# Retention stage of a hybrid layer rebuilt: one lag table, GLU tiles between the heads, column sums, and an out projection begun with the state-space half

## The reference

```python
def ab_mixer(...):        # layer 0
    ql, kl, vl, gl, ul = jnp.split(h_lat @ w_in, cuts, axis=-1)
    r = retention_mixer(...)      # 4 heads of 128; decay exp(log_gamma * |i-j|), both directions, latents start
                                  # from the context's state; rms over the head; times silu(g)
    s = s5_mixer(...)             # 32 groups of a diagonal state space, then gelu, then GLU:
                                  #   y * sigmoid(y @ glu_w + glu_b)
    return jnp.concatenate([r, s], axis=-1) @ w_out
```

## Time and profile before

| | us |
|---|---|
| median of 3 runs (1980.96 to 1985.2) | 1985.0 |
| the profiled execution's own time | 1991.38 |
| its span, first to last instruction | 1989.6 |
| TensorE busy in it | 1875.2 (94%) |
| VectorE busy | 1226.2 (62%) |
| ScalarE busy | 733.2 (37%) |
| last `ab_out` matmul ends, from the start of the span | 761.5 |

### The profile page before, as it was taken

The page is one execution under the profiler, slowest core; times in us unless marked ns, Lnnn a source line. Parts: engine busy times, 40 slices in busy tenths (PEclk is TensorE's granted clock), DMA queues, the critical chain, the costliest instruction groups (busy, mean ns, idle before and its releaser), DMA issues.

```text
span 1989.6 us, 25349 instructions
## 1 busy us (share of the span) xinstructions
PE 1875.2 (94%) x9624; PEld 1557.9 (78%) x9624; DVE 1226.2 (62%) x2021; ACT 733.2 (37%) x1006; POOL 62.6 (3%) x39
## 2 busy tenths in 40 slices
PE   6999999999886689999999999999999999989998
PEld 2788888877786367888888778888887996689998
DVE  4777567779998454776676377764334334545554
ACT  2432122247666434322132342212224323444443
POOL 0000000110000010000000200000010000010001
PEclk8999999989998798999999999999998998989999
DMA  7454454321100122543553344443222520024543
GB/s 288 164 196 152 181 200 179 113 86 64 43 33 33 53 89 81 211 179 142 199 196 120 113 162 178 167 169 127 87 82 85 207 90 1 1 106 148 185 175 126
DMA packets 39859, 259.10 MB, mean 130 GB/s; under 512 B 4688, under 2 KB 5840, under 8 KB 14704
## 3 DMA queue, kind: packets, MB, share of 16 engines
q1 hardware_dynamic: 39792, 258.23, 35.5%
HBM read 257.17 MB, written 1.05 MB: 130 GB/s over the span
## 4 chain that ended last, share of the span: by engine, by line
PE 84%; DVE 10%; ACT 3%; issue 2%; DMA 1%; SPq 0%; DVEq 0%; ACTq 0%
PE ps_all L1528 25%; PE ps_all L1532 25%; PE ps_all L1529 25%; PE ps_all L1840 2%; PE bank L1851 2%; DVE w_lo L914 2%; PE bank L1576 1%; DMA start_scale<-in_w_scale 1%; PE ps_all L1830 1%; PE bank L1830 1%; ACT w_hi L551 1%; PE bank L1879 1%; DVE cp L444 1%; PE bank L1770 1%; DVE stat L1289 1%
## 5 line engine op out<-in xcount | busy, mean ns | idle before, releaser
L1528 PE MATMUL ps_all<-a_hi,w_lo 128*128 128x512 f32 (+1 forms) x1808 | 666.3, 369 | 29.0 <-ACT a_hi L659 14.0
L1532 PE MATMUL ps_all<-a_lo,w_hi 128*128 128x512 f32 (+1 forms) x1808 | 661.1, 366 | 0.2 <-DVE a_lo L1053 0.2
L1529 PE MATMUL ps_all<-a_hi,w_hi 128*128 128x512 f32 (+1 forms) x1808 | 660.7, 365 | 0.0
L914 DVE TENSOR_TENSOR w_lo<-w_raw,w_hi 128x2048 fp32r<-128x2048 f32 (+3 forms) x184 | 376.3, 2045 | 169.5 <-ACT w_hi L551 168.3
L551 ACT ACTIVATE w_hi<-w_raw 128x2048 fp32r<-128x2048 f32 (+3 forms) x183 | 313.5, 1713 | 350.0 <-PE ps_all L1532 347.0
L1528 PEld LDWEIGHTS ps_all<-a_hi,w_lo 128*128 128x128 f32 x1808 | 347.3, 192 | 88.8 <-issue 16.1
L1532 PEld LDWEIGHTS ps_all<-a_lo,w_hi 128*128 128x128 f32 x1808 | 347.0, 192 | 57.1 <-DVE a_lo L1053 4.1
L1529 PEld LDWEIGHTS ps_all<-a_hi,w_hi 128*128 128x128 f32 x1808 | 347.7, 192 | 52.2
L926 DVE SCALAR_TENSOR_TENSOR mod_junk<-mod_raw,cond 128x1024 bf16<-128x1024 f32 x256 | 302.5, 1218 | 4.7 <-ACT cond L579 2.7
L1528 PE MATMUL ps_all<-g_hi,w_lo 128*128 128x512 f32 (+1 forms) x704 | 258.3, 367 | 0.8 <-DVE w_lo L914 0.8
L1532 PE MATMUL ps_all<-g_lo,w_hi 128*128 128x512 f32 (+1 forms) x704 | 258.1, 367 | 0.0
(11 more groups left out here) (209 smaller groups left out, 1564.7 us busy)
## 6 DMA issues: line engine op xcount, KB each, us to landing
w_raw<-in_tiles SPq DMA_DIRECT2D x118, 1024.0 KB, 4.8
mod_raw<-in_w_mod SPq DMA_DIRECT2D x64, 1024.0 KB, 4.8
w_raw<-in_tiles SPq DMA_DIRECT2D x32, 768.0 KB, 4.0
w_raw<-in_tiles SPq DMA_DIRECT2D x32, 640.0 KB, 3.7
start_raw<-in_w_mod SPq DMA_DIRECT2D x4, 1024.0 KB, 16.0
start_scale<-in_w_scale SPq DMA_DIRECT2D x4, 1024.0 KB, 20.1
bias<-in_na_bias SPq DMA_DIRECT2D x2, 1536.0 KB, 8.3
cond<-in_cond SPq DMA_DIRECT2D x2, 1024.0 KB, 6.0
```

The costliest lines, as they stand in the source:

```text
L914: nc.vector.tensor_tensor(w_lo[:, slot, 0:size], w_raw[:, slot, 0:size], w_hi[:, slot, 0:size].bitcast(F32), ALU.subtract).then_inc(lo_rea ...
L1528: pe.matmul(dst, w[1], x[0], start=start, stop=False)
L1529: pe.matmul(dst, w[0], x[0], start=False, stop=False)
L1532: return pe.matmul(dst, w[0], x[1], start=False, stop=stop_)
```

## The change

- One plane of lags i-j (512 wide, `lag`) replaces the six. It is loaded before the loop, the logits earlier still, and log_gamma is worked out beside ffn0.down1. For each head: decay[:,0] = exp(min(lf*d, -lb*d)) plus the identity on the diagonal blocks, and the cross term exp(lf*d + 256 lf) + exp(-lb*d + 256 lb), so three exponentials and one scaled copy on ScalarE, and one min, one add and two 128-wide adds on VectorE. Each head has buffers of its own, so that ScalarE no longer waits for VectorE's masks.
- In the loop ScalarE does gelu(2b-1) ahead of the kernel rows; the last gate tile is evacuated one turn earlier; in turn 7 VectorE's split of the second `glu` weights moves from ahead of rotate(15) to behind the split of y, and the scores of head 0 go between the last two outputs.
- The `glu` tiles run between the heads, tile 1 into bank[2] and bank[0]; the scores go to ps[1] and bank[1].
- The sum of squares is a column sum (16 matmuls with one column for each of the four heads' 4 blocks), one Sqrt over 16 columns, one reciprocal, and a spread by four 128-wide matmuls a head.
- `ab_out` tiles 0 and 1 begin with the state-space half of k; heads lie in a_hi blocks 4 to 7, y in 0 to 3. Both first weights are split ahead of the tail's end.

```diff
@@ SyncE
             if segment == "ffn0.down0":
+                sp.dma_start(lgam, i["decay"]).then_inc(ret_sem["gam_in"], 16)
             if segment == "ret_in":
+                sp.wait_ge(pe_done, BASE["s5_in"])
+                sp.dma_start(lag[:], i["lags"]).then_inc(ret_sem["loads"], 16)
...
-                if segment == "glu":
-                    sp.wait_ge(s5_sem["y"], 16)
-                    sp.dma_start(lags[:].rearrange("p a b -> p (a b)"), i["lags"]).then_inc(ret_sem["loads"], 16)
-                    sp.dma_start(lgam[:], i["decay"]).then_inc(ret_sem["loads"], 16)
@@ ScalarE
+                def exponentials(hd):
+                    nc.scalar.activation(decay_of[hd][:, 1, :], lag[:], ACT.Exp, bias=lg[5][:, hd:hd + 1], scale=lg[3][:, hd:hd + 1])
+                    nc.scalar.activation(cross_of[hd], lag[:], ACT.Exp, bias=lg[5][:, 4 + hd:5 + hd],
+                                         scale=lg[4][:, 4 + hd:5 + hd]).then_inc(R["cross"], 1)
+                    act.wait_ge(R["least"], hd + 1)
+                    nc.scalar.activation(decay_of[hd][:, 0, :], decay_of[hd][:, 0, :], ACT.Exp).then_inc(R["exp2"], 1)
...
                 for b in range(8):
+                    if b:
+                        gelu(2 * b - 1)
                     kernel_rows(2 * b)
                     kernel_rows(2 * b + 1)
-                    if b:
-                        gelu(2 * b - 1)
...
+                    if b == 7:
+                        act.wait_ge(S["c"], 8)
+                        slopes(0)
                     gelu(2 * b)
...
                         evacuate(6)
+                        evacuate(7)
+                exponentials(0)
                 gelu(15)
-                evacuate(7)
...
+                for hd in range(1, 4):
+                    slopes(hd)
+                    exponentials(hd)
+                keep(0)
+                split_hi(BASE["ab_out"], 2048, 0)
+                sigmoids(0)
+                keep(1)
+                keep(2)
+                sigmoids(1)
+                split_hi(BASE["ab_out"] + 1, 2048, 1)
+                nc.scalar.activation(warm[:], eps[:], ACT.Sqrt)
+                keep(3)
+                act.wait_ge(R["sum"], 4)
+                nc.scalar.activation(hstd[:], bank[1][:, 0:16], ACT.Sqrt, bias=eps[:, 0:1], scale=D / P).then_inc(R["std"], 1)
                 for hd in range(4):
+                    act.wait_ge(R["mixed"], hd + 1)
+                    nc.scalar.activation(a_hi[:, 4 + hd, :], heads[:, hd, :], ACT.Copy).then_inc(R["cast"], 1)
@@ VectorE
+                mask(0)
+                weigh(0)
                 dve.wait_ge(S["gelu"], 16)
...
+                split_lo(BASE["glu"] + 1, width("glu"), 1)
+                mask(1)
+                weigh(1)
+                mask(2)
+                mask(3)
+                weigh(2)
+                split_lo(BASE["ab_out"], 2048, 0)
+                gated_head(0)
+                weigh(3)
+                y_mix(0)
+                gated_head(1)
+                gated_head(2)
+                y_mix(1)
+                split_lo(BASE["ab_out"] + 1, 2048, 1)
+                gated_head(3)
+                dve.wait_ge(R["std"], 1)
+                nc.vector.reciprocal(hrstd[:], hstd[:]).then_inc(R["rstd"], 1)
@@ TensorE
+                    else:                              # b == 7, after outputs(14)
...
+                        head_scores(0)
                     outputs(2 * b + 1)
...
+                head_scores(1)
+                head_out(0)
+                pe.wait_ge(R["y_split"], 1)
+                glu_tile(0)
+                head_scores(2)
+                head_out(1)
+                head_scores(3)
+                head_out(2)
+                pe.wait_ge(S["rot"], 16)
                 pe.wait_ge(S["gelu"], 16)
...
+                glu_tile(1)
+                head_out(3)
+                pe.wait_ge(R["p"], 4)
                 for hd in range(4):
...
+                    head_sum(hd)
+                out_tile(0, (4, 5))
+                pe.wait_ge(ps_free[1], (BASE["glu"] + 1) // 2 + 1)
+                head_spread(0)
+                head_spread(1)
+                out_tile(0, (6, 7))
+                head_spread(2)
+                pe.wait_ge(R["std"], 1)
+                head_spread(3)
+                out_tile(1, (4, 5, 6, 7))
+                out_tile(0, (0, 1, 2, 3))
+                out_tile(1, (0, 1, 2, 3))
+                for j in range(2, 4):
+                    pair_tile_from("ab_out", j)
```

More of the change, by code:

```diff
@@ L330, in program @@
         ret_sem = {n: sem("ret_" + n) for n in (
-            "loads", "qk", "swapped", "rope", "exp1", "exp2", "gam", "mask", "s", "p", "o", "osq", "kept", "sum", "ln", "std",
-            "y_split", "mix")}
+            "loads", "gam_in", "qk", "swapped", "rope", "gam", "exp1", "slope", "least", "cross", "exp2", "mask", "s", "p", "o",
+            "osq", "kept", "gated", "sum", "std", "rstd", "spread", "mixed", "cast", "mix", "y_split", "ymix")}
         na_sem = {n: sem("na_" + n) for n in (
@@ L606, in step @@
                 def step(t, slot, first=False):
-                    if not (isinstance(t, int) and t == tiles - 1):
+                    if segment == "ab_out" and t == 0:
+                        pass
+                    elif not (isinstance(t, int) and t == tiles - 1):
                         split_hi(BASE[segment] + t + 1, width(segment), 1 - slot)
@@ new lines, in head_out, with head_sum @@
+                def head_out(hd):
+                    pe.wait_ge(R["p"], hd + 1)
+                    if hd:
+                        pe.wait_ge(R["kept"], hd)
+                    for t in (0, 2, 3, 1):
+                        b = 0 if t < 2 else 256
+                        mm = pe.matmul(ps_sum[:, b:512], vtok[:, t, hd * P:(hd + 1) * P], scores[:, t, b:512],
+                                       start=(t == 0), stop=(t == 1))
+                    mm.then_inc(R["o"], 1)
+                def head_sum(hd):
+                    pe.wait_ge(R["osq"], hd + 1)
+                    for t in range(4):
+                        mm = pe.matmul(bank[1][:, 4 * hd + t:4 * hd + t + 1], hsq[hd][:, t * P:(t + 1) * P], mean_c[:],
+                                       start=True, stop=True)
+                    mm.then_inc(R["sum"], 1)
@@ new lines, in head_spread @@
+                def head_spread(hd):
+                    pe.wait_ge(R["rstd"], 1)
+                    if hd == 2:
+                        pe.wait_ge(R["kept"], 4)
+                    for t in range(4):
+                        mm = pe.matmul(spread_to[hd][:, t * P:(t + 1) * P],
+                                       hrstd[:, 4 * hd + t:4 * hd + t + 1].broadcast_to([P, P]),
+                                       const[:, C_IDENT:C_IDENT + P], start=True, stop=True)
+                    mm.then_inc(R["spread"], 1)
@@ new lines, in out_tile @@
+                def out_tile(j, ks):
+                    n = BASE["ab_out"] + j
+                    pe.wait_ge(lo_ready, n + 1)
+                    pe.wait_ge(ps_free[j], n // 2)
+                    w = [x[:, j].rearrange("p (k m f) -> p k m f", k=KT, m=2) for x in (w_hi, w_lo)]
+                    for k in ks:
+                        if k < 4:
+                            pe.wait_ge(R["mix"], k + 1)
+                        else:
+                            pe.wait_ge(R["ymix"], k - 3)
+                        for m in range(2):
+                            mm = three(ps[j][:, m, :], [x[:, k, m] for x in w], (a_hi[:, (k + 4) % 8, :], a_lo[:, (k + 4) % 8, :]),
+                                       k == 4, k == 3)
+                    if k == 3:
+                        mm.then_inc(pe_done, 1)
@@ L1775, in mixer0 @@
-                head_sum(3)
-                pe.wait_ge(R["ln"], 4)
-                pe.wait_ge(R["y_split"], 1)
-                for j in range(2):
-                    pair_tile("glu", j, 4, 4)
-                for j in range(4):
-                    pair_tile("ab_out", j, 8, 0, lambda k: pe.wait_ge(R["mix"], k + 1) if j == 0 else None)
+                head_scores(1)
[3 more added lines that the diff above has]
+                head_scores(2)
```

247 lines of the change are left out of this document (127 added, 120 removed).

## The result

The changed kernel takes 1958.4 us (median of 4 runs, 1958.26 to 1960.32); the kernel before, run on the same chip beside it, took 1985.1 (4 runs, 1980.96 to 1989.07). The ratio is 0.9858, with a 95% interval of 0.9839 to 0.9877, so 1.4% faster. The prediction was 1956.0, with a range from 1947 to 1970.

What follows compares the result with a forecast made beforehand. TensorE, 94% busy, bounds the kernel; only 78 of the mixer tail's 115 us are work. Tail 29.2 plus loop 1.5 is 30.7, minus 1.7 for handoffs gives 29: 1985 - 29 = 1956, range 1947 to 1970.

Steps and rivals of the forecast that it cites:

- The loop: Loop turn 5: VectorE's split no longer waits 1.46 us for ScalarE's w_hi, as gelu moves into idle time; -1.5.
- Moved preparation: Small operations and loads moved to ffn0.down1 fit beside busy TensorE; cost 0, or 2 us without that cover.
- Steps 1 to 3: Tail's start: turn_back(15) done at 640.5 instead of 644.4, outputs(15) ends at 643.0, p1 at 645.8, before 664.2.
- Steps 4 to 6: Tail's heads: scores 1 take 4.2 after 2.8 idle, `glu` tile 0 without a wait, one 2.1 us gap left.
- Step 7: Tail from 666.1: scores 3 through `ab_out` without a break, 66.2 us, ending at 732.3.
- the 1.7 us taken off for handoffs: Taken off the summed 30.7 us gain for some twenty handoffs of nearly 0.1 each left out; leaves 29.
- five signs of the text: New trace: p1 near 644, last `ab_out` matmul near 731, one 2 us idle, no w_hi wait, half clock until about 650.
- A: Tail: short gaps keep TensorE's clock down from scores 1 to value product 2, 21 us more, 1977; chance 0.12.
- B: Tail's heads: product, keep and weigh stay serial, nothing of `glu` hidden; +6.4, 1962; chance 0.13.
- C: Tail: VectorE and ScalarE are always early, the full bound, 1947 to 1950; chance 0.07.
- D: Tail: waits for p2, kept and p3 bring the clock down, `ab_out` stays cold; 53 more, 2038; chance 0.02.
- E: Tail's start: some new wait holds it, only hidden `glu` tiles and first split gained; 1970; chance 0.06.

Runs made afterwards that it cites:

- two edits: Changed kernel plus a second buffer for weighed scores (two heads in flight) and column sums laid between first `ab_out` blocks: 1952.3 us, ratio 0.9813.

## Why the prediction was right

Predicted for the difference was 29.0 us, measured 27.85 in the stage and 26.7 in the medians. By its steps, in positions 0.7 us later than it gave them (turn 0 is 2.2 later, turn 5 took off 1.5):

- **The loop, -1.5.** -1.43 from the split of turn 4 to that of turn 5, and the wait came back when the order was undone.
- **Moved preparation, 0.** Held: turn 0 starts at 468.10 in one execution of the changed kernel, and TensorE was busy throughout where the preparation lies.
- **Steps 1 to 3.** turn_back(15) 641.3 (predicted 641.2), outputs(15) 643.1 (643.7), p1 646.63 (646.5). The whole ordering of ScalarE and VectorE in turn 7 held, down to the table switches: gelu(14) ended at 640.75, and the load behind it took 1.28 with the next operation 1.30 after its start. The drain that the Trainium skill adds ("ScalarE: Activation LUTs", What ACT_TABLE_LOAD costs) isn't there, and the 3 us later end that it gave did not come.
- **Steps 4 to 6.** Scores 1 took 4.37 (4.2) after 3.61 us idle (2.8), scores 2 waited for nothing, kept head 0 was ready at 660.9, 0.8 before TensorE asked, and the one gap was 2.08 (2.1).
- **Step 7, mis-sized.** Predicted were 66.2 us from scores 3 to the end, measured 69.3 (666.53 to 735.83). Scores 3 cost 4.37, not 3.6 (in the kernel before, such a set took 4.00, from 673.88 to 677.88, after 2.17 us idle, as the row below shows in part: I had priced only its first four matmuls from there); the column sums 4.47, not 3.6; `ab_out` 46.2, not 43.6, for half clock at its start; the spreads 3.6, not 4.4. The step says "from 666.1 TensorE has work without a break", which was so, and took from it that the clock stays up, which was not so. That the forecast came this close is in part luck: the 1.7 us taken off for handoffs covered for more than half of this error, and no such handoffs show in step 7, where TensorE is busy for 5.00 of every 5 us from 676 to 691.

```profile
676.18 1.91 PE L1753 MATMUL bank<-qk 128*128 128x256 f32 x4
```

- **No wait for ymix, mix or kept.** None came. Of the five signs of the text, three held: p1 (644.4 in the positions of before), the one idle gap, and no wait for w_hi in turn 5. Two did not. The last `ab_out` matmul came at 733.6 in those positions, not near 731; and instead of "half-clock matmuls only up to about 650" they came again at 666.5 to 671 and from about 684 to 691.
- **A reading of the rows.** The prediction says that the clock line of the earlier trace rows dips to 6 to 8 tenths, and only where TensorE waits. The line has nothing under 7, and the changed kernel's column sums show a dip without a wait. Step 7 accordingly has no price for what the sums do to the clock.

The rivals: A had the right place and not the size. The low clock lasted for the scores behind both gaps, 1.8 us each, and was back at 1.00 in the next window, instead of holding through 23 us. So the pattern of the Trainium skill, short gaps that swing the clock ("TensorE: Matmul & The Clock Gate", A second HAM failure mode: psum-queue depth-cycling), is in the trace twice, at 1.8 us a time. B did not happen: value product 3 ended at 681.7, not 688, though without `glu` tile 0 as cover 3.3 us came back. C was not reached; what separates it from the changed kernel is mostly the 7.5 us that two edits take away. Of D, the cause (a low clock at the start of `ab_out`) came true, with 2.4 us lost where it needed 29, and behind the column sums, not behind the waits that it named. E did not happen.

What I had not known: the choice to begin with the state-space half, which looked like a main part of the change, is worth about 0.5 us, because column roots leave hardly anything to hide.

## What to carry to other kernels

Look at what stands behind the last producer of a stage: here 20 of 28 us were won before the first product, most of them, as the chains of waits have it, by work (the load of the lag table, exponentials, a split) that only waited for its turn there and could be done earlier. When a TensorE gap is closed, look for two gains, the idle time and the low clock that can follow it. And keep runs of one-column matmuls short: put them between wide ones.

## What the hardware showed that I had not expected

- A run of 32 one-column fp32 matmul instructions brought TensorE's granted clock down without a single idle moment: 0.82 in the window with most of the sums and 0.50 in the next, 0.59 even when TensorE had been busy at 1.00 for 40 us before. The same matmuls, eight or sixteen at a time with six 512-column ones between, left it at 1.00. It costs 1.2 us in the sums and 2.4 in the work behind. What it is in them (the one column, or the many short instructions) was not tried.
- The same idle gap does not always have the same price. After 2.08 or 2.09 us idle the four wide score matmuls took 1.99, 2.45, 3.06, 3.09, 3.15, 3.19 and 3.47 in seven kernels; after 2.31 and 2.63 they took 1.98, but after 2.13 in another kernel 3.73; after 3.59 to 3.61 in five kernels 3.62 to 3.68. What sets it in the short gaps stays open.
- VectorE's reciprocal takes 3.35 us for 128x512, against 0.69 for a multiplication.
